# Delta-rule systems written to device memory whole, head by head, their diagonal blocks read back at once; the weight unit after the last head split ahead of that head's transfer

## The reference, cut to what matters

```python
a_mat = jnp.where(strict, bc[..., :, None] * kk * decay, 0.0)
rhs = jnp.concatenate([bc[..., None] * vc, (bc * jnp.exp(gc))[..., None] * kc], axis=-1)
sol = lax.linalg.triangular_solve(a_mat + eye, rhs, left_side=True, lower=True,
                                  unit_diagonal=True)
```

## Time and profile before

| | us |
|---|---|
| median of 3 runs (lowest, highest) | 2737.89 (2735.12, 2739.23) |
| the profiled execution's own time | 2732.86 |
| its span | 2731.2 |
| PE busy | 2670.1, 98% of the span |
| DVE busy | 2156.4, 79% |
| ACT busy | 1424.8, 52% |
| mean granted TensorE clock | 0.998 of full speed |
| the stretch around the change: head 0 to the first level of products | 366 to 429 from the span's start |

### The profile page before, as it was taken

How to read it: one execution, slowest core, us unless ns; L and a number is a source line. 1 busy time by engine, 2 the same in 40 slices (tenths; PEclk the granted TensorE clock), 3 DMA queues, 4 the chain that set the end, 5 groups by cost and what they waited for, 6 DMA issues and landing times.

```text
span 2731.2 us, 51117 instructions
## 1 busy us (share of the span) xinstructions
PE 2670.1 (98%) x18740; PEld 2410.3 (88%) x18740; DVE 2156.4 (79%) x3979; ACT 1424.8 (52%) x2239; POOL 131.8 (5%) x202
## 2 busy tenths in 40 slices
PE   6999999999999999999999999999999999999999
PEld 6999888899999999988888888899999988888887
DVE  6888885688876768888889887666588888898665
ACT  4555554455545455555544455555555555544454
POOL 0113130001010000000000010000000000000000
PEclk9999999999999999999999999999999999999999
DMA  8885462488775555555555688544555555555554
GB/s 326 313 308 195 147 219 72 143 291 313 255 279 184 194 183 186 182 171 174 165 176 174 212 292 289 189 163 162 169 186 185 178 170 171 170 172 176 187 194 152
DMA packets 157513, 550.84 MB, mean 202 GB/s; under 512 B 23280, under 2 KB 23792, under 8 KB 157040
## 3 DMA queue, kind: packets, MB, share of 16 engines
q1 hardware_dynamic: 131136, 464.64, 50.2%
q0 software_dynamic: 22176, 80.75, 8.7%
q10 hardware_dynamic: 3984, 2.45, 0.3%
HBM read 546.33 MB, written 1.44 MB: 201 GB/s over the span
## 4 chain that ended last, share of the span: by engine, by line
PE 77%; PEld 10%; DVE 7%; DMA 3%; issue 2%; ACT 1%; PEldq 0%; SPq 0%; ACTq 0%; DVEq 0%
PE acc L2665 17%; PE acc L2672 8%; PE acc L2045 8%; PE st L2045 6%; PE st L2032 6%; PE st L2036 6%; PE st L2033 6%; PE acc L2049 4%; PE st L2049 3%; DVE w_lo L1044 3%; PE st L2632 2%; DMA ring<-weights 2%; PEld acc L2032 1%; PEld acc L2036 1%; PEld acc L2033 1%
## 5 line engine op out<-in xcount | busy, mean ns | idle before, releaser
L1044 DVE TENSOR_TENSOR w_lo<-ring,w_hi 128x1024 fp32r<-128x1024 f32 x860 | 1055.8, 1230 | 382.2 <-ACT w_hi L536 148.0
L536 ACT ACTIVATE w_hi<-ring 128x1024 fp32r<-128x1024 f32 x860 | 900.7, 1052 | 272.1 <-DMA ring<-weights 161.4
L2032 PE MATMUL st<-h_both,w_hi 128*128 128x256 f32 x1680 | 415.7, 285 | 1.5 <-ACT arena L945 1.2
L2033 PE MATMUL st<-h_both,w_hi 128*128 128x256 f32 x1680 | 412.2, 283 | 0.0
L2032 PEld LDWEIGHTS st<-h_both,w_hi 128*128 128x128 f32 x1680 | 321.5, 191 | 9.6 <-issue 5.1
L2033 PEld LDWEIGHTS st<-h_both,w_hi 128*128 128x128 f32 x1680 | 321.8, 192 | 0.1
L2665 PE MATMUL acc<-w_hi,act_hi 128*128 128x512 f32 x1016 | 318.8, 395 | 0.0
L2665 PE MATMUL acc<-w_hi,act_lo 128*128 128x512 f32 x1016 | 313.1, 389 | 0.0
L986 ACT ACTIVATE act_hi<-arena 128x256 fp32r<-128x256 f32 x256 | 106.8, 418 | 374.3 <-PE acc L2672 370.0
L2045 PE MATMUL st<-h_both,w_hi 128*128 128x512 f32 x1184 | 297.1, 393 | 0.5 <-ACT w_hi L536 0.5
L2672 PE MATMUL acc<-w_lo,act_hi 128*128 128x512 f32 x1016 | 271.5, 389 | 0.0
(11 more groups left out here) (373 smaller groups left out, 3730.2 us busy)
## 6 DMA issues: line engine op xcount, KB each, us to landing
ring<-weights SPq DMA_DIRECT2D x864, 512.0 KB, 3.4
arena<-ada_weights POOLq DMA_DIRECT2D x104, 512.0 KB, 5.7
extra<-ada_weights POOLq DMA_DIRECT2D x48, 512.0 KB, 4.7
arena<-ada_weights SPq DMA_DIRECT2D x16, 512.0 KB, 13.4
arena<-const ACTq DMA_DIRECT2D x1, 1280.0 KB, 7.6
x_t<-params SPq DMA_DIRECT2D x1, 1024.0 KB, 11.5
extra<-crows POOLq DMA_DIRECT2D x2, 512.0 KB, 5.2
out<-arena SPq DMA_DIRECT2D x4, 256.0 KB, 2.1
```

What stands on the lines that cost most here:

```text
L536: nc_a.activation(w_hi[:, u % 3, :], ring[:, u % RING, :], ACT.Copy).then_inc(hi_ready, 1)
L1044: v.tensor_tensor(w_lo[:, u % 2, :], ring[:, u % RING, :], w_hi[:, u % 3, :], ALU.subtract)\
L2032: mm(dst(t), w, hi_t(t), start=start, stop=False, skip_group_check=True)
L2033: mm(dst(t), w, lo_t(t), start=False, stop=False, skip_group_check=True)
```

## The change

Device memory `blocks` now holds whole systems: for each of the 16 systems eight block rows of 16 x 129 values, of which 128 x 128 values are written row by row (`rows_of`), so that the diagonal blocks are found by one regular pattern in them (`diagonal_of`). The blocks in `sub_u` are now ordered by system and then by block, and so is `inverses`.

SP handles each head as it ends: it issues the load of unit 107 + h, waits for `head` to say h + 1, issues one DMA of 64 KB for each of the head's two systems, waits for both to land, and issues one DMA for the diagonal blocks of each. The second system of head 7 is left to ACT, with its own semaphore `last_in`. ACT does `hi(112)` before that, where it stood behind the four DMAs before. DVE waits for the blocks after `fill(16)` instead of after `fill(17)`, and the runs of elimination steps are 4, 4, 4, 3. The load of units up to 119 still stands ahead of the write of the inverses on SP.

```diff
-SUB_STEPS = (3, 4, 4, 4)
+SUB_STEPS = (4, 4, 4, 3)
...
+BLOCKS_IN = 16 * (4 * (HEADS - 1) + 2)
+BLOCKS_OUT = BLOCKS_IN + 16
...
+        def rows_of(n):
+
+            return blocks[n, 0:P * P].rearrange("(p i) -> p i", i=P)
+
+        def diagonal_of(n):
+
+            return blocks[n, :].rearrange("(b r) -> b r", b=N_SUB)[:, 0:SUB * P]\
+                .rearrange("b (j i) -> b j i", i=P)[:, :, 0:SUB]
...
-            last_head = (U_MIX + N_QKV + FILL_AT[HEADS - 1]) // RING + 1
-            turns_of(1, last_head)
-            unit(last_head * RING)
-            unit(last_head * RING + 1)
-            eng = sp
-            eng.wait_ge(sem("head"), HEADS)
-            for k in range(N_SUB // 2):
-                at = slice(SUB * k, SUB * k + SUB)
-                eng.dma_start(blocks[k].rearrange("n j i -> j n i"), a_t[at, :, at]).then_inc(sem("blocks"), 16)
-            eng.wait_ge(sem("blocks"), 16 * N_SUB)
-            eng.dma_start(sub_u.rearrange("p j i -> p (j i)"), blocks.rearrange("b n j i -> (b n) (j i)"))\
-               .then_inc(sem("blocks"), 16)
-            unit(last_head * RING + 2)
+            first_fill = U_MIX + N_QKV + FILL_AT[0] + 4
+            turns_of(1, (first_fill - 1) // RING)
+            for u in range((first_fill - 1) // RING * RING, first_fill):
+                unit(u)
+            for h in range(HEADS):
+                unit(first_fill + h)
+                sp.wait_ge(sem("head"), h + 1)
+                of_head = (h, HEADS + h) if h < HEADS - 1 else (h,)
+                for n in of_head:
+                    sp.dma_start(rows_of(n), a_t[:, n, :]).then_inc(sem("blocks"), 16)
+                sp.wait_ge(sem("blocks"), 64 * h + 16 * len(of_head))
+                for n in of_head:
+                    sp.dma_start(sub_u[N_SUB * n:N_SUB * (n + 1), :, :], diagonal_of(n)).then_inc(sem("blocks"), 16)
+            for u in range(first_fill + HEADS, (first_fill + HEADS) // RING * RING + RING):
+                unit(u)
             solve = (U_POOLP + 2) // RING
-            turns_of(last_head + 1, solve)
-            eng.wait_ge(sem("inv_done"), 1)
...
+            turns_of((first_fill + HEADS) // RING + 1, solve)
+            sp.wait_ge(sem("inv_done"), 1)
...
-            def diagonal_blocks():
-
+            def last_system():
+
+                n = 2 * HEADS - 1
                 eng.wait_ge(sem("head"), HEADS)
-                for k in range(N_SUB // 2, N_SUB):
-                    at = slice(SUB * k, SUB * k + SUB)
-                    eng.dma_start(blocks[k].rearrange("n j i -> j n i"), a_t[at, :, at]).then_inc(sem("blocks"), 16)
+                eng.dma_start(rows_of(n), a_t[:, n, :]).then_inc(sem("last_in"), 16)
+                eng.wait_ge(sem("last_in"), 16)
+                eng.dma_start(sub_u[N_SUB * n:N_SUB * (n + 1), :, :], diagonal_of(n)).then_inc(sem("last_in"), 16)
...
                 if h == HEADS - 1:
-                    diagonal_blocks()
+                    hi(U_MIX + N_QKV + FILL_AT[h] + 2)
+                    last_system()
...
             fill(FILL_AT[HEADS - 1])
-            fill(FILL_AT[HEADS - 1] + 1)
             eng.wait_ge(sem("lv_ready"), 1)
-            eng.wait_ge(sem("blocks"), 16 * (N_SUB + 1))
+            eng.wait_ge(sem("blocks"), BLOCKS_IN)
+            eng.wait_ge(sem("last_in"), 32)
...
                 if n < len(SUB_STEPS) - 1:
-                    fill(FILL_AT[HEADS - 1] + 2 + n)
+                    fill(FILL_AT[HEADS - 1] + 1 + n)
             v.tensor_copy(sub_vt, sub_v.rearrange("p j i -> p i j")).then_inc(sem("inv_done"), 1)
-            for f in range(FILL_AT[HEADS - 1] + 1 + len(SUB_STEPS), N_FILL):
+            for f in range(FILL_AT[HEADS - 1] + len(SUB_STEPS), N_FILL):
```

More of the change, by code:

```diff
@@ L492, in _ @@
-            eng.wait_ge(sem("blocks"), 16 * N_SUB)
-            eng.dma_start(sub_u.rearrange("p j i -> p (j i)"), blocks.rearrange("b n j i -> (b n) (j i)"))\
-               .then_inc(sem("blocks"), 16)
-            unit(last_head * RING + 2)
-            solve = (U_POOLP + 2) // RING
-            turns_of(last_head + 1, solve)
-            eng.wait_ge(sem("inv_done"), 1)
-            eng.dma_start(inverses.rearrange("b n s j i -> (b n) (s j i)"), ar(1536, 2 * SUB * SUB))\
-               .then_inc(sem("blocks"), 16)
@@ L501, in _ @@
-            eng.wait_ge(sem("blocks"), 16 * (N_SUB + 2))
-            eng.wait_ge(sem("lv_ready"), 1)
+            first_fill = U_MIX + N_QKV + FILL_AT[0] + 4
[11 more added lines that the diff above has]
+                    sp.dma_start(sub_u[N_SUB * n:N_SUB * (n + 1), :, :], diagonal_of(n)).then_inc(sem("blocks"), 16)
@@ new lines, in _ @@
+            for u in range(first_fill + HEADS, (first_fill + HEADS) // RING * RING + RING):
+                unit(u)
+            solve = (U_POOLP + 2) // RING
+            turns_of((first_fill + HEADS) // RING + 1, solve)
+            sp.wait_ge(sem("inv_done"), 1)
+            sp.dma_start(inverses.rearrange("n b s j i -> (n b) (s j i)"), ar(1536, 2 * SUB * SUB))\
+              .then_inc(sem("blocks"), 16)
+            sp.wait_ge(sem("blocks"), BLOCKS_OUT)
+            sp.wait_ge(sem("lv_ready"), 1)
@@ L503, in _ @@
             for k in range(N_SUB):
                 at = slice(SUB * k, SUB * k + SUB)
-                eng.dma_start(d_m[at, :, at], inverses[k, :, 1, :, :].rearrange("n j i -> j n i"))\
-                   .then_inc(sem("blocks"), 16)
+                sp.dma_start(d_m[at, :, at], inverses[:, k, 1, :, :].rearrange("n j i -> j n i"))\
+                  .then_inc(sem("blocks"), 16)
             turns_of(solve, N_UNITS // RING)
@@ L729, in _ @@
             link(nc_a.activation(nbe, g_col[:, 1, :], ACT.Exp))
-            def diagonal_blocks():
+            def last_system():
+                n = 2 * HEADS - 1
                 eng.wait_ge(sem("head"), HEADS)
-                for k in range(N_SUB // 2, N_SUB):
-                    at = slice(SUB * k, SUB * k + SUB)
-                    eng.dma_start(blocks[k].rearrange("n j i -> j n i"), a_t[at, :, at]).then_inc(sem("blocks"), 16)
+                eng.dma_start(rows_of(n), a_t[:, n, :]).then_inc(sem("last_in"), 16)
+                eng.wait_ge(sem("last_in"), 16)
+                eng.dma_start(sub_u[N_SUB * n:N_SUB * (n + 1), :, :], diagonal_of(n)).then_inc(sem("last_in"), 16)
             def inverses_by_row():
-                eng.wait_ge(sem("blocks"), 16 * (N_SUB + 2))
+                eng.wait_ge(sem("blocks"), BLOCKS_OUT)
                 eng.wait_ge(sem("lv_ready"), 1)
@@ L742, in inverses_by_row @@
                     at = slice(SUB * k, SUB * k + SUB)
-                    eng.dma_start(d_t[at, :, at], inverses[k, :, 0, :, :].rearrange("n j i -> j n i"))\
+                    eng.dma_start(d_t[at, :, at], inverses[:, k, 0, :, :].rearrange("n j i -> j n i"))\
                        .then_inc(sem("blocks"), 16)
@@ L2327, in _ @@
             ins.then_inc(sem("pool_mm"), 1)
-            eng.wait_ge(sem("blocks"), 16 * (3 * N_SUB + 2))
+            eng.wait_ge(sem("blocks"), BLOCKS_OUT + 16 * 2 * N_SUB)
             for lv in range(len(LEVELS)):
@@ L2840 @@
     out = nc.dram_tensor("out", (P, DT * T), F32, kind="ExternalOutput").ap()
-    blocks = nc.dram_tensor("blocks", (N_SUB, 16, SUB, SUB), F32, kind="Internal").ap()
-    inverses = nc.dram_tensor("inverses", (N_SUB, 16, 2, SUB, SUB), F32, kind="Internal").ap()
+    blocks = nc.dram_tensor("blocks", (2 * HEADS, N_SUB * SUB * (P + 1)), F32, kind="Internal").ap()
+    inverses = nc.dram_tensor("inverses", (2 * HEADS, N_SUB, 2, SUB, SUB), F32, kind="Internal").ap()
     build(nc, *args, blocks, inverses, out)
```

## The result

The changed kernel takes 2742.47 us in the median of 20 runs (2736.73 to 2745.56), the kernel before 2737.86 in its 20 (2734.93 to 2740.55). The medians lie 4.6 us apart. The ratio is 1.0014, with a 95% interval of 1.0008 to 1.0021, which is 3.8 us: slower by less than the 0.2% that was set as telling, but more than nothing. The forecast was 2739.9, with a range of 2733.5 to 2744.5.

The account below looks back on a forecast made before the run. PE is busy 98%; the start of the first level (line 2336), set by the chain of waits, decides. -1.25 + 0 + 3.3 + 0 = +2.05 us on the median 2737.89 gives 2739.9, range 2733.5 to 2744.5.

Parts of the forecast that it names:

- part 1: Up to the elimination's start: no longer held by lo(113), now set by the blocks; 1.25 us earlier than before.
- part 3: Copy to inverses in memory: SP held by lo(116), then inverses land behind unit 119's 512 KB; costs 3.3 us.
- rival B: SP's ring falls behind the heads, turns of 6.9 us, DVE and PE stop 3 us; 2744 us, chance 0.12.
- T: Start of the elimination on DVE: 409.85 us before the change, forecast at 408.6.
- The rule: On SP's queue a head's systems land 0.45 us after the unit ahead of them, not overtaking it.
- it holds, barely: Late units in the heads still reach ACT in time, with margins of 0.4 to 1.5 us; counted as nothing.
- B's point of decision: Unit landing of about 4.9 us in the first three turns, from which the ring falls behind the heads.
- Part 2: Elimination start to copy: same 15 steps and three fills, runs of 4, 4, 4, 3; costs nothing.
- rival A: On SP's queue small transfers overtake the units: elimination at 404.4, -3.7 us in sum, 2734.2 us; chance 0.20.
- Part 4: Inverses in memory to first level: transfers back take 5.75 us as before; PE has about 3 us of cover.

Follow-up runs that it names:

- the second execution: The changed kernel, unaltered, run and profiled once more beside the kernel before; 2742.82 us, ratio 1.0014.
- the best kernel: Changed kernel with SP reading diagonal blocks one turn later and writing the inverses ahead of unit 119; 2729.46 us, ratio 0.9975.

## Why the forecast held, and where its working failed

The forecast of no telling change held, the direction (+2.05 us) too, and the waits that decided were those of parts 1 and 3. The size was about half of what was measured (4.6 us by the medians, 3.8 by the ratio), and by the trace part 1 is where it went wrong.

That the number held is in part luck. The traces have +3.9 us in part 1 and +3.6 in part 3, so the first level starts 7.5 us later than before, where +2.05 was forecast. Added to the median before, 7.5 us would be 2745.4, outside the range; the timed runs show only 4.6 of it. The measured 2742.5 also lies just outside the forecast's own 2738 to 2742, towards rival B.

**Part 1, when the elimination starts: wrong sign.** The forecast had T = 38.4 us after head 0, 1.25 earlier than before. The traces have 43.9 and 43.3, 3.9 later. The rule was right for the late turns: the systems land after the unit ahead of them, which the kernel with the unit behind them shows by its 2.0 us against 3.75, and they land 0.45 us behind it, as taken (398.5 to 398.95). What was mis-sized is the length of the turns. Against head 0, T came 5.5 us later than forecast. Most of it, 3.7 us, is in the three early turns: 7.3, 6.7 and 6.3 us, where 5.8, 5.8 and 5.0 were taken (in the second execution 5.7, 6.9 and 6.1). Another 1.0 us is in the three late ones, 4.8 instead of 4.45, since the unit itself took 3.7 us where 3.2 was taken. Why it did is open: without the reads ahead of it, it still took 3.5 to 3.9. The first early turn is long by its unit, which took 6.2 us to land. In the next two, from 381.78 and 388.49, the systems landed 2.3 and 1.9 us behind the unit and not 0.45, and the second execution has 2.4 and 2.0 in the same two turns. Why is open; they were not the work of GpSimd's loads alone, as the last of these had landed by 387.5.

**The units in the heads: "it holds, barely" did not.** This is rival B, mild in the heads, though T came later than even B had it (43.9 us after head 0, against 411.7 - 370.2 = 41.5). ACT waited for ring loads in heads 3, 5, 6 and 7 (0.6, 1.8, 3.2 and 2.8 us), and head 7 ended 1.3 us later against head 0, where B had 3. B's point of decision was a landing of 4.9 us in the first turns; one of 6.2 us was there.

**Part 2, runs of steps: right.** 10.65 us from start to copy, as before.

**Part 3, the inverses: right.** Forecast 3.3 us; 22.6 against 19.0 is 3.6. SP issued them 2.1 us behind the copy's start, against 0.4 before, and they landed in 4.1 us. That the inverses landed in under 2.5 us once unit 119 stood behind them speaks against rival A, in which small transfers overtake. The Trainium skill (DMA: Bandwidth & Descriptors, Queues, rings and completion order) says that each DMA engine takes the descriptors of one ring in order. The landings of the inverses and the late turns with the unit behind the systems agree with it.

**Part 4, PE's cover: right.** PE still waited 2.7 and 2.6 us, a little under the 3 to 5 taken, and the clock fell as before (first 32 recorded products 5.3 us; before has 5.3, 6.5 and 5.5 in its three executions).

So the change did free the elimination from unit 113, worth about 4 us by the kernel before with that load and the split of unit 112 moved (35.5 against 39.7), and spent it twice: in SP's turns and behind unit 119. Undoing both costs gives 13.7 us in the trace (82.2 against 95.9) and 10.7 us in ratio (0.9975 against 1.0014).

## What to carry to other kernels

Before small transfers are put into the queue of a streaming engine, write the turn of that queue as a sum: the load ahead, its landing, the wait, the issues; if it is longer than the period of the work, the last item comes late by the whole difference times the number of turns. Let such a queue not wait for a transfer that it has just issued: here the read one turn later brought the elimination 9 us forward with the same bytes. So read one turn later, and issue the transfer on which others wait ahead of the large load. And look first for the one load that is merely issued late: moving two ring loads ahead of one wait, with the split of unit 112, gave 0.21% where the best kernel has 0.25%, with no new transfers. The intervals of the two overlap.

## What the runs showed of the hardware

- Two systems of 64 KB landed 2.0 us after the first issue with a 512 KB load right behind it on the same queue, and 3.75 us with that load ahead, in late turns of the head loop. In five earlier turns they took 2.3 to 4.6 us with the load behind them.
- 256 KB landed in 2.2 us when issued 2.0 us behind a 512 KB load, and in 4.1 us when issued 0.5 us behind one.
- The granted clock fell around PE's wait before the first level: with waits of 3.7, 4.0, 4.1 and 4.3 us the first 32 recorded products took 5.3, 6.5, 6.3 and 6.6 us. With a wait of 1.4 us or less they took 3.8. Between, at 2.1 to 2.8 us, both were seen: 5.3 to 5.5 in five executions and 3.8 in two. In those two the clock fell some 26 us later: the first 16 recorded products of line 2371, behind a wait of 0.8 us as in every execution, took 3.6 us instead of 2.05, at a granted clock down to 0.50.
